# Modulation weights in the mixing stage: four chunks multiplied ahead of the gate units, the others one behind each unit

## What is computed

```
modulation(cvec) = split(silu(cvec) @ w_ada + b_ada, 6)         # w_ada is 1024 x 6144
h    = rmsnorm(x) * (1 + scale_m) + shift_m
z    = h @ w_in                                                 # -> u, q, k, v, gate_a, gate_b; w_in is 1024 x 4096
a    = pool_mixer(u) @ w_pa
o    = attention(q, k, v) @ w_pb                                # latent tokens also attend to cached keys
x    = x + gt_m * ((sigmoid(gate_a) * a + sigmoid(gate_b) * o) @ w_out)
h    = rmsnorm(x) * (1 + scale_f) + shift_f
x    = x + gt_f * top-4-of-32 clamped-SwiGLU experts(h)         # w_up 1024 x 2048, w_down 1024 x 1024, each of 32
y    = rmsnorm(x)
```

## Time and profile before

| | |
|---|---|
| time, median of 3 runs | 1139.18 us (1138.95 to 1139.79) |
| the profiled execution's own time | 1139.19 us |
| its span, first to last instruction | 1137.2 us |
| TensorE busy | 1064.5 us (94%) |
| VectorE, ScalarE, GpSimd busy | 331.8, 168.8, 66.7 us |
| bytes moved | 459.36 MB, mean 404 GB/s |
| mean granted TensorE clock | 0.987 |

### The profile page before, as it was taken

One profiled execution on the slowest core, in us unless ns is written; L12 is line 12 of the kernel. 1 busy time (PEld: TensorE's weight loads), 2 busy tenths in 40 slices (PEclk: granted clock), 3 DMA queues, 4 the chain that ended last, 5 costly groups with the idle time before them and its releaser, 6 DMA issues.

```text
span 1137.2 us, 14086 instructions
## 1 busy us (share of the span) xinstructions
PE 1064.5 (94%) x5882; PEld 504.6 (44%) x5882; DVE 331.8 (29%) x622; ACT 168.8 (15%) x302; POOL 66.7 (6%) x107
## 2 busy tenths in 40 slices
PE   7999899999999998989899999898989899998996
PEld 6877699843333333333333333333333333333332
DVE  4776777522121212121212111212121212121113
ACT  4453135510000000000000000000000000000001
POOL 5050000200000000000000000000000000000000
PEclk9999999999999999999999999999999999999999
DMA  9998987899999999999999999999999999999995
GB/s 308 376 259 328 384 294 311 343 418 424 429 427 428 437 427 434 430 430 433 427 433 432 431 435 428 437 428 432 433 430 436 428 413 431 435 432 424 429 426 239
DMA packets 44487, 459.36 MB, mean 404 GB/s; under 512 B 3716, under 2 KB 16072, under 8 KB 26936
## 3 DMA queue, kind: packets, MB, share of 16 engines
q1 hardware_dynamic: 42808, 455.12, 95.9%
q0 software_dynamic: 1168, 2.81, 1.0%
q10 hardware_dynamic: 464, 0.79, 0.2%
HBM read 457.12 MB, written 1.57 MB: 403 GB/s over the span
## 4 chain that ended last, share of the span: by engine, by line
DMA 48%; PE 45%; DVE 2%; SPq 2%; issue 1%; ACT 1%; POOL 1%; POOLq 0%; DVEq 0%; ACTq 0%
DMA arena<-in_w_down_dram 39%; PE ps L1801 20%; PE ps L1762 12%; DMA ring<-in_w_up_dram 4%; DMA ring<-in_w_in_dram 3%; PE ps L1790 2%; PE ps L1742 1%; DMA ring<-in_w_ada_dram 1%; DMA ring<-in_rpb_dram 1%; SPq L429 1%; PE ps L1492 1%; SPq L425 1%; PE ps L1493 1%; PE ps L1663 1%; PE ps L1494 1%
## 5 line engine op out<-in xcount | busy, mean ns | idle before, releaser
L1762 PE MATMUL ps<-ring,arena 128*64 128x512 f32 x2048 | 453.7, 594 | 5.5 <-DMA ring<-in_w_up_dram 5.4
L1801 PE MATMUL ps<-arena,x 128*64 128x512 f32 x992 | 231.9, 622 | 42.4 <-DMA arena<-in_w_down_dram 42.4
L1762 PEld LDWEIGHTS ps<-ring,arena 128*64 128x64 f32 x2048 | 142.7, 137 | 273.8 <-issue 258.6
L1801 PEld LDWEIGHTS ps<-arena,x 128*64 128x64 f32 x992 | 73.6, 143 | 199.0 <-issue 143.7
L1301 DVE TENSOR_SCALAR x<-ps 128x512 f32<-128x512 f32 x32 | 22.1, 691 | 255.2 <-PE ps L1762 255.2
L1294 DVE TENSOR_SCALAR arena<-iota,cur 128x128 f32<-128x128 f32 x64 | 19.3, 344 | 260.2 <-PE ps L1772 260.0
L1316 DVE TENSOR_TENSOR late<-ps,gtf 128x512 f32<-128x512 f32 x64 | 41.2, 686 | 180.5 <-PE ps L1801 180.5
L654 POOL COPY selbuf<-sel 96x64 bf16 (+1 forms) x32 | 24.5, 766 | 841.9 <-DVE x L1302 839.5
L1790 PE MATMUL ps<-late,arena 64*128 64x512 f32 x264 | 65.6, 615 | 1.5 <-DVE late L1316 1.5
L878 ACT ACTIVATE x<-x 128x512 f32<-128x512 f32 x32 | 20.2, 630 | 283.8 <-DVE x L1301 283.8
L1742 PE MATMUL ps<-arena 128*128 128x128 f32 x496 | 60.7, 276 | 0.0
(11 more groups left out here) (272 smaller groups left out, 862.6 us busy)
## 6 DMA issues: line engine op xcount, KB each, us to landing
ring<-in_w_up_dram SPq DMA_DIRECT2D x51, 4096.0 KB, 29.2
arena<-in_w_down_dram SPq DMA_DIRECT2D x24, 4096.0 KB, 20.5
ring<-in_w_up_dram SPq DMA_DIRECT2D x25, 2048.0 KB, 12.2
arena<-in_w_down_dram SPq DMA_DIRECT2D x13, 2048.0 KB, 18.2
ring<-in_w_ada_dram SPq DMA_DIRECT2D x16, 1024.0 KB, 10.6
ring<-in_w_ada_dram SPq DMA_DIRECT2D x16, 512.0 KB, 10.1
ring<-in_w_in_dram SPq DMA_DIRECT2D x16, 512.0 KB, 9.7
ring<-in_w_in_dram SPq DMA_DIRECT2D x8, 1024.0 KB, 8.0
```

The costliest lines, as they stand in the source:

```text
L1762: ins = mm(ps[CAP * h:CAP * h + CAP, half, :].rearrange("q (p j) -> q p j", j=4), xgT[:, place, kk, CAP * a:CAP * a + CAP], w[:, half, :, ...
L1801: ins = mm(ps[CAP * n:CAP * n + CAP, YB, :], hT[:, j, CAP * h:CAP * h + CAP], w[:, jj, n * HALF:(n + 1) * HALF], start=(jj == 0), stop=(jj ...
```

## The change

Four ada chunks (0 to 3) are multiplied ahead of gate unit 0, between the steps that stand there; the other twelve follow one behind each of units 0 to 11. The accumulation in bank 3 now starts earlier, so the v projection's second half moves to bank 6 (`V_BANK`), and the wait for its read-out stands before the scores that write banks 6 and 7. VectorE takes the row of chunks 0 to 7 out before `split(6)`, no longer after `split(7)`. Slots and load order are written anew.

```
-    whole("in", 5, range(2), [1, 10])
-    whole("ada", 1, range(4, 8), [11, 2, 0, 3])
-    whole("ada", 2, range(2), [11, 2])
-    whole("in", 6, range(2), [0, 3])
-    whole("ada", 2, range(2, 6), [10, 11, 1, 2])
-    whole("in", 7, range(2), [10, 11])
-    whole("ada", 2, range(6, 8), [1, 0])
+    whole("in", 5, range(2), [1, 2])
+    whole("ada", 1, range(4, 8), [0, 3, 10, 11])
+    whole("ada", 2, range(1), [0])
+    whole("in", 6, range(2), [3, 10])
+    whole("ada", 2, range(1, 5), [11, 1, 2, 0])
+    whole("in", 7, range(2), [11, 1])
+    whole("ada", 2, range(5, 8), [2, 0, 3])
...
-ADA_AFTER = [1, 1, 2] * 4 + [0] * 4
+ADA_FIRST = 4
+ADA_AFTER = [1] * 12 + [0] * 4
...
+            mod_rows(1)
             split(6)
             split(7)
-            mod_rows(1)
...
+            modulation(0)
             pe.wait_ge(bias_copied, 1)
             scores(0, kT[:, :, 0:P], 4)
+            modulation(1)
             pe.wait_ge(yT_ready, 1)
...
             ins.then_inc(kc_t, 1)
+            modulation(2)
             pe.wait_ge(row_ready, 4)
             pe.wait_ge(A_ready, 4)
+            pe.wait_ge(z_read, 4)
             scores(1, kT[:, :, P:TOK], 6)
+            modulation(3)
             pe.wait_ge(kcT_ready, 1)
             gates(0, 1, 2, 3)
```

More of the change, by code:

```diff
@@ L386, in layer_kernel @@
         NT = [(n, t) for n in range(2) for t in range(2)]
+        V_BANK = (2, 6)
         AF_BANK, GT_BANK = (0, 1, 2, 3), (4, 7)
@@ L727, in z_out @@
                 for b in range(2):
-                    src = ps[:, bank + b, :]
+                    src = ps[:, V_BANK[b] if cc == 3 else bank + b, :]
                     if cc == 0:
@@ L1399, in modulation @@
                     m, kk = 1 + k // KB, k % KB
-                    if k == 0:
-                        pe.wait_ge(z_read, 4)
                     if k == KB:
@@ L1475, in project_v @@
                         kk, c = 2 * q + a, slice(t * P, (t + 1) * P)
-                        mm(ps[:, 2 + t, :], hT_top[:, kk, c], early_top[:, n % 3, a, :], start=(kk == 0), stop=False)
-                        mm(ps[:, 2 + t, :], hT_rest[:, kk, c], early_top[:, n % 3, a, :], start=False, stop=False)
-                        ins = mm(ps[:, 2 + t, :], hT_top[:, kk, c], early_rest[:, n % 3, a, :],
+                        mm(ps[:, V_BANK[t], :], hT_top[:, kk, c], early_top[:, n % 3, a, :], start=(kk == 0), stop=False)
+                        mm(ps[:, V_BANK[t], :], hT_rest[:, kk, c], early_top[:, n % 3, a, :], start=False, stop=False)
+                        ins = mm(ps[:, V_BANK[t], :], hT_top[:, kk, c], early_rest[:, n % 3, a, :],
                                  start=False, stop=(kk == KB - 1))
                 ins.then_inc(early_used, 1)
-            done = [0]
+            done = [ADA_FIRST]
             def gates(*units):
```

## The result

The changed kernel is slower: 1151.05 us median of 5 runs (1149.74 to 1152.54) against 1139.79 (1138.95 to 1141.87), a ratio of 1.0095 (95% interval 1.008 to 1.011). The direction was forecast, and so were the waits for chunks 6, 8 and 10; the time lies above the range, whose upper end was 1148.3. The profiled execution is the quickest of the five, 1149.74 us; its span is 1147.9, 10.7 more than before.

A forecast was written before the change was run, and what follows sets the result against it. TensorE's way through the gate units was taken as the bound. From 1139.2 us, new waits of 9.57 less 5.45 gone (+4.1) and two slow-clock stretches (+3.0) gave 1146.3 us, range 1142.1 to 1148.3.

The forecast's parts named there:

- What bounds the kernel: Whole kernel: TensorE's way through the gate units sets the end; a microsecond there is a microsecond at the end.
- The matmuls that move: TensorE, gate units: the same sixteen chunks cost the same, only waits change; the extra z_read wait is free.
- what goes: TensorE's old idle times, for split(8), chunks 4, 14 and 15 and the pool mixer's output, vanish: 5.45 us.
- The last load: Second half of w_pa, waiting for split(15): lands about 157.9, wanted at 158.76, hidden; costs up to 0.7 us if slower.
- Chunk 6: TensorE behind unit 2: waits 3.56 us, since slot 10 comes back only after split(3); bounds 3.5 to 4.4.
- chunk 10: TensorE behind unit 6: waits 3.56 us, since slot 1 is given back only by split(7).
- Chunk 8: TensorE behind unit 4: waits 1.05 us for VectorE to take out the row of chunks 0 to 7; bounds 0.8 to 1.3.
- Chunk 4: TensorE ahead of unit 1: waits 1.4 us for a load third in line, landing about 89.7; bounds 0.3 to 2.2.
- The clock: TensorE behind the waits for chunks 6 and 10: slow clock costs 1.5 us each, +3.0 us, bounds 0 to 3.4.
- Quick landings: Rival: the modulation's late loads land in 4.4 us, waits shrink, 1140.3 us; chance 0.07.
- DMA-bound: Rival: the DMA stream bounds the stage, only chunk 8's 1.05 us wait stays, 1134.8 us; chance 0.05.
- the edit not doing what it says: Rival: chunk 3 must have landed by its turn at 84.2; put at 81.4 at most, no wait; no chance given.

The follow-up runs named there:

- the kernel with two ahead: Changed kernel with two chunks ahead of the units, one behind units 0 to 11, two behind 12, rows taken later, two slots swapped: 1136.15 us, ratio 0.9961.
- the run that had them alone: Changed kernel with the v cache store later, GpSimd's b_up loads behind chunk 4, chunk 5's load behind those of chunks 6 and 7: 1156.43 us, one run.
- the fill run: Changed kernel with 13, 10 and 9 identity matmuls ahead of chunks 4, 6 and 10, to keep TensorE at work: 1147.54 us, ratio 1.0057.
- the pairs: Changed kernel with chunks 6 and 7 both behind unit 3, chunks 10 and 11 both behind unit 7: 1147.81 us, ratio 1.006.

## Why the prediction failed, and where it held

**What bounds the kernel.** Right. TensorE's way through the units passed to the end nearly whole: 10.0 us at the first load of w_up, 10.7 in the span, 11.3 by the medians. In the kernel with two ahead 5.2 us at the units became 4.3 by the medians, and 2.8 in the spans of the two profiles (1137.2 and 1134.4), so not all of it was seen to arrive.

**The matmuls that move, and what goes.** Right. All five old waits are gone, the two matmul orders cost the same, the z_read wait nothing. The last load, of w_pa, went out at 162.4 and ScalarE's first branch unit started at 168.75, right behind what it does ahead of it: hidden, as forecast.

**Chunk 6 and chunk 10.** The mechanism is right, the size 17% high: 3.12 and 2.96 us for 3.56. A chunk with nothing ahead landed after 5.0 us, not 5.4. The Trainium skill's fit for loads that GpSimd issues (DMA: Bandwidth & Descriptors, Anatomy of one DMA; about 2.0 us and 436 GB/s, an estimate of 4.4 us for 1 MB) was still too short: alone, loads of 1 MB that SP issues took 4.8 to 5.4 here.

**Chunk 8.** 0.98 us for 1.05. **Chunk 9** had 0.17 us that the working did not look for: it followed the loads of chunks 4, 6 and 10 one by one, and left this one out.

**Chunk 4, the step that failed.** It was taken at 1.4 us, at most 2.2, and measured 3.90. Its terms were a first load of 5.3 us and 2.4 us from load to load, both from rows in which loads went out 0.4 us apart or into an idle DMA. The landings in the changed kernel, for the issues at 79.67, 81.76 and 83.34:

```profile
ring<-in_w_in_dram SPq DMA_DIRECT2D x1, 1024.0 KB, 6.9
...
ring<-in_w_in_dram SPq DMA_DIRECT2D x1, 1024.0 KB, 8.1
...
ring<-in_w_ada_dram SPq DMA_DIRECT2D x1, 1024.0 KB, 9.0
```

They are 86.6, 89.9 and 92.3, for 84.9, 87.3 and 89.7. By the run that had them alone they would be near 85.1, 88.8 and 91.3. So the term that failed is the 2.4 us from the first load to the second, which was 3.8, 1.4 us too little; the store of the v cache, for which the upper bound had 0.8 us, added 1.0 to chunk 4. GpSimd's loads made the first load late and not chunk 4. The prediction said that the DMA has little to do between 80 and 91 us. The trace of the kernel before shows that this begins somewhat later than 79.7, where the first load now goes out:

```profile
76.00:80.00 4.00, 3.63 (x28) 2.83 (x26) 1.15 (x2) 2.51 (x6) 3.28 (x6) 1.00 1.01 181
80.00:84.00 4.00, 3.80 (x37) 3.51 (x38) 2.67 (x4) 3.23 (x10) 2.05 (x4) 1.00 0.35 90
```

The Trainium skill (DMA: Bandwidth & Descriptors, Issuing engines are not separate DMA queues) says that DMAs issued by different engines run on the same 16 DMA engines and interleave; the runs agree: the first load took 6.9 us beside GpSimd's, 5.4 without the last three of them.

**The clock.** Two slow stretches were priced, 1.5 us each, behind chunks 6 and 10. There were two, but behind chunk 4, where 6.8 us passed at 1.2 GHz and cost 2.44 us, and behind chunk 10, 1.54 us; 4.0 us for 3.0, and the fill run gives 3.5 to 4.3. None was priced behind chunk 4 because its wait was taken at 1.4 us, and no wait of 1.6 us or less had had one. So that one term is 2.5 us of wait and 2.4 us of clock, 4.9 us; chunks 6 and 10 together are 1.0 us below their sum, and no slow stretch followed chunk 6, 1.5 below. Together with the 0.2 us of chunk 9 this makes 1146.3 into some 1149, and the profiled execution took 1149.74. The median is 1.3 us above that execution, and the kernel before had 1139.79 in the same rounds, 0.6 more than the prediction started from.

**The range.** Its upper end, 1148.3, took waits of 5.7 us with both slow stretches. The prediction's own bounds, 7 us of waits and 3.4 of clock, add up to 1149.6; the low bounds of its terms add up to 2.7 us, not 2.9. The median lies above even the wider sum.

**The rivals.** Quick landings, DMA-bound and the edit not doing what it says are all out. Of the two waits priced with a slow stretch one, for chunk 6, had none; the second slow stretch was the one behind chunk 4, which nothing in the prediction names. That the DMA stream is the bound is refuted by the kernel with two ahead, too, where the same stream lets the units pass without a wait.

## What to carry to other kernels

When work is pulled ahead, count for each load behind it the time from the release of its slot to its use, and ask for the longest of landing, not the median: a chunk moved one unit up takes its wait from the chunk's own release, and a second load in the same burst needs 2.5 us more, or some 4 in the bad case. Look at what other engines have in flight when a released load goes out. A wait on the engine that sets the pace can cost its length and the slow clock behind it too: here 19 of 25 waits of 2.88 us and more had one, and it was a third of the loss.

## What the runs showed of the hardware

A load of 1 MB into an idle DMA landed after 4.8 to 5.4 us. In a burst, the next ones followed at steps of 2.4 to 2.7 us, but for single steps of 3.0 to 4.6 us. The traces show what those go with, which the runs above had not been made for. Ten of the twelve kernels issue four loads within 1.3 to 2.2 us when the slots of in 4 come free, chunks 6, 7, 8 and the first half of in 6 (6, 7, 5 and 8 where chunk 5 is held). In seven of them one step among the four took 3.5 to 4.0 us, each time the one in which a 16 KB packet of the instruction queue passed (at 109.7 us in the changed kernel, between chunks 7 and 8; at 105.5 with the pairs, between 6 and 7). In the other three, the fill run among them (packet at 97.7 us, before the loads went out), the packet fell elsewhere and no step was over 2.7 us; nor was one in any of the ten among chunks 10, 11, 12 and the first half of in 7, which no packet met. Chunk 8 from issue to landing, in the changed kernel and in the fill run:

```profile
ring<-in_w_ada_dram SPq DMA_DIRECT2D x1, 1024.0 KB, 10.3
...
ring<-in_w_ada_dram SPq DMA_DIRECT2D x1, 1024.0 KB, 9.0
```

For the loads ahead of chunk 4 the packet came at 84.4 to 85.5 us in all eleven kernels with this change, as the first two loads were on their way. So it is the likely reason of the 1.4 us, but no run has this burst without it, and no run moved the packet on purpose.

In the nine changed kernels with such waits, six timed and three run once, the profiles hold 25 waits of 2.88 us and more of TensorE in this stage. Behind 19 of them, or towards their end, the granted clock fell to 1.2 GHz. That is all nine of 3.20 us and more, and 10 of the 16 from 2.88 to 3.12 us; among these the length did not decide, as 2.88 us had it and 3.12 did not. Behind none of 0.9 to 1.5 us did it. The slow stretch was 3.4 us, which cost 1.5 us where it fell on a chunk and a unit; or 6.8 where the last 1.0 us and more of the wait lay in it, which cost 2.4 to 2.6. The two waits of 12 us had stretches of 13.7 and 10.2 us.
